# Where a head of the prompt's sparse attention ends and the next begins: last projection tile cut in two, query transposes and first scores moved into the next head's first tile

## What is computed

```python
def block(args):                     # _dsa_attention, one block of 128 queries
    qq, qqi, ww, qp = args
    rel = jax.nn.relu(jnp.einsum('bqhd,bsd->bqhs', qqi, ki).astype(jnp.float32))
    score = jnp.einsum('bqhs,bqh->bqs', rel, ww.astype(jnp.float32))
    score = jnp.where(vis[None], score, -jnp.inf)
    _, idx = lax.top_k(score, topk)
    ...
    s = jnp.einsum('bqngd,bqknd->bqngk', qq.reshape(b, qb, hkv, g, d), kg) * scale
    pr = jax.nn.softmax(jnp.where(ok[:, :, None, None, :], s, -jnp.inf), axis=-1)
    o = jnp.einsum('bqngk,bqknd->bqngd', pr.astype(v.dtype), vg)
ob = ob.reshape(b, t, D_B) * jax.nn.silu(gs)      # gate of each head, from the same input projection
```

## Time and profile before

| | us |
|---|---|
| median of three timed runs | 3538.22 |
| timed runs, lowest to highest | 3528.4 to 3543.82 |
| the profiled execution, its own time | 3525.9 |
| its span, first to last instruction | 3524.3 |
| TensorE busy in the span | 3332.7 (95%) |
| this stage, first product to the next stage's first | 1735.5 to 2491.3 |
| projections of this stage (line 1588), TensorE busy | 383.3 + 86.7 |

### The profile page before, as it was taken

One profiled execution on the slowest core, in us unless ns is written; L12 is line 12 of the kernel. 1 busy time (PEld: TensorE's weight loads), 2 busy tenths in 40 slices (PEclk: granted clock), 3 DMA queues, 4 the chain that ended last, 5 costly groups with the idle time before them and its releaser, 6 DMA issues. The chain is left out here.

```text
span 3524.3 us, 45823 instructions
## 1 busy us (share of the span) xinstructions
PE 3332.7 (95%) x17235; PEld 2281.7 (65%) x17265; DVE 1553.3 (44%) x2769; ACT 810.9 (23%) x1781; POOL 778.0 (22%) x992
## 2 busy tenths in 40 slices
PE   5878999999999999999999999999999998999999
PEld 3666777777777677777788888887444444444443
DVE  2025887878777787765434553112000023111111
ACT  4011233333425242433112222222100002000000
POOL 0005664646474655540000001000000000000000
PEclk8989999999999999999999999999999999999999
DMA  9866496878686877764301111103111023021010
GB/s 344 251 204 180 147 293 214 288 229 295 213 294 215 271 245 267 237 222 145 114 24 31 40 41 47 42 7 121 47 48 44 5 84 103 33 72 66 24 63 24
DMA packets 315102, 496.39 MB, mean 141 GB/s; under 512 B 26113, under 2 KB 211738, under 8 KB 313714
## 3 DMA queue, kind: packets, MB, share of 16 engines
q1 hardware_dynamic: 264512, 338.50, 30.1%
q0 software_dynamic: 46592, 146.84, 12.3%
q10 hardware_dynamic: 3778, 8.13, 0.6%
HBM read 466.02 MB, written 27.37 MB: 140 GB/s over the span
## 5 line engine op out<-in xcount | busy, mean ns | idle before, releaser
L1277 PE MATMUL Z<-W,hT 128*128 128x256 f32 x4608 | 1061.9, 385 | 16.7 <-DMA W<-in_w_in_dram 13.7
L1277 PEld LDWEIGHTS Z<-W,hT 128*128 128x128 f32 x4608 | 860.3, 191 | 173.8 <-issue 46.4
L2173 PE MATMUL S<-W,hT 128*128 128x512 f32 x1408 | 646.6, 597 | 1.8 <-SPq L2130 1.8
L2173 PEld LDWEIGHTS S<-W,hT 128*128 128x128 f32 x1408 | 265.1, 191 | 350.1 <-issue 347.3
L1588 PE MATMUL DB<-W,hT 128*128 128x256 f32 x1696 | 383.3, 381 | 0.0
L1588 PEld LDWEIGHTS DB<-W,hT 128*128 128x128 f32 x1696 | 316.3, 190 | 39.9
L996 DVE TENSOR_REDUCE sc<-big 128x16 f32<-128x1024 f32 x256 | 309.4, 1208 | 2.2 <-POOL big L816 1.7
L2173 PE MATMUL Z<-W,hT 128*128 128x512 f32 x640 | 303.6, 592 | 0.0
L992 DVE TENSOR_TENSOR big<-big,qb 128x1024 f32<-128x1024 f32 x160 | 231.8, 1449 | 76.4 <-DMA big<-in_cache_diff_k_dram 74.1
L816 POOL TENSOR_TENSOR big<-big,qb 128x1024 f32<-128x1024 f32 x96 | 231.3, 2410 | 101.9 <-DMA big<-in_cache_diff_k_dram 100.9
L2173 PEld LDWEIGHTS Z<-W,hT 128*128 128x128 f32 x640 | 121.5, 190 | 153.0 <-issue 152.6
(11 more groups left out here) (525 smaller groups left out, 3201.8 us busy)
## 6 DMA issues: line engine op xcount, KB each, us to landing
big<-in_cache_diff_k_dram POOLq DMA_DIRECT2D x256, 512.0 KB, 5.1
big<-in_cache_diff_v_dram SPq DMA_DIRECT2D x256, 512.0 KB, 4.6
W<-in_w_in_dram SPq DMA_DIRECT2D x27, 2048.0 KB, 9.9
W<-in_w_in_dram SPq DMA_DIRECT2D x52, 1024.0 KB, 8.1
W<-in_w_ple_gate_dram SPq DMA_DIRECT2D x16, 1024.0 KB
W<-in_w_out_dram SPq DMA_DIRECT2D x12, 1024.0 KB
kib<-in_cache_idx_k_dram POOLq DMA_DIRECT2D x256, 32.0 KB, 2.7
hT<-oT_d SPq DMA_DIRECT2D x3, 2048.0 KB, 20.4
```

The costliest lines, as they stand in the source:

```text
L1277: mm = pe.matmul(Z[b][:, 0:CW], hT[:, k, t * P:(t + 1) * P], W[:, w, k, :], start=(k == 0), stop=(k == KT - 1))
L2173: mm = pe.matmul(b, hT[:, k, t * P:(t + 1) * P], Wr[:, k, :], start=(k == 0), stop=(k == KT - 1))
```

## The change

Lists of three engines are written in a new order; no operation is added or taken away, and no semaphore. On TensorE:

- Tile 6 keeps only the first half of tile 7's projection; its two points `sample(point(s, 6, 0))` and `sample(point(s, 6, 1))` now follow each other. The second half stands in tile 7, behind `probabilities(H, 7, 0)`, and after it follow point, `probabilities(H, 7, 1)`, point, `output(H, 7)`.
- The next step begins with `half(s, 0, 0)`, then `queries(H)`, `turned(H - 1, 0)`, `half(s, 0, 1)`, `scores(H, 0)`, `turned(H - 1, 1)`, the point, `half(s, 1, 0)`, and only then the wait for the first exponentials, `probabilities(H, 0, 0)`, `scores(H, 1)`, `half(s, 1, 1)`, point, `output(H, 0)`.
- The last step (`s` = 8) has no next head, so these pieces stand there without the half tiles.

ScalarE takes tile 7 out of its bank in tile 7, between the two copies of probabilities, and copies the queries, the turned outputs and tile 0 before the first exponentials. VectorE rotates the queries in tile 7 between its two points, and makes the first maximum, the gates' product and point (s, 0, 0) ahead of the first tile.

```diff
-        ahead = lambda s, t: () if s == HB else ((t,) if s == 0 else ((0, 1) if t == 0 else ((t + 1,) if t < NT - 1 else ())))
+        ahead = lambda s, t: () if s == HB else ((0, 1) if t == 0 else ((t + 1,) if t < NT - 1 else ()))
...
-                for f in range(parts(t)):
-                    count_t += 1
-                    TN[s - 1, t, f] = count_t
                 if t == 0 and s >= 2:
                     for f in range(2):
                         count_t += 1
                         OG[s - 2, f] = count_t
+                for f in range(parts(t)):
+                    count_t += 1
+                    TN[s - 1, t, f] = count_t
...
                         half(0, t, f)
                         sample(point(0, t, f))
-                queries(0)
-                scores(0, 0)
                 for s in range(1, HB + 1):
                     H = s - 1
-                    for t in range(NT):
+                    if s < HB:
+                        half(s, 0, 0)
+                    queries(H)
+                    if s >= 2:
+                        turned(H - 1, 0)
+                    if s < HB:
+                        half(s, 0, 1)
+                    scores(H, 0)
+                    if s >= 2:
+                        turned(H - 1, 1)
+                    sample(point(s, 0, 0))
+                    if s < HB:
+                        half(s, 1, 0)
+                    pe.wait_ge(h_x, NT * H + 1)
+                    probabilities(H, 0, 0)
+                    scores(H, 1)
+                    if s < HB:
+                        half(s, 1, 1)
+                    sample(point(s, 0, 1))
+                    output(H, 0)
+                    for t in range(1, NT):
                         pe.wait_ge(h_x, NT * H + t + 1)
                         probabilities(H, t, 0)
                         if t < NT - 1:
                             scores(H, t + 1)
-                        elif s < HB:
-                            queries(s)
-                        if parts(t) > 1:
+                            if parts(t) > 1:
+                                probabilities(H, t, 1)
+                            if s < HB:
+                                half(s, t + 1, 0)
+                            sample(point(s, t, 0))
+                            if s < HB and t < NT - 2:
+                                half(s, t + 1, 1)
+                        else:
+                            if s < HB:
+                                half(s, t, 1)
+                            sample(point(s, t, 0))
                             probabilities(H, t, 1)
-                        if t == 0 and s >= 2:
-                            turned(H - 1, 0)
-                        for c in ahead(s, t):
-                            half(s, c, 0)
-                            if c != 1:
-                                sample(point(s, t, 0))
-                                if c == 0 and s >= 2:
-                                    turned(H - 1, 1)
-                            half(s, c, 1)
-                        if not ahead(s, t):
-                            if t == 0 and s >= 2:
-                                turned(H - 1, 1)
-                            sample(point(s, t, 0))
-                            if t == NT - 1 and s < HB:
-                                scores(s, 0)
                         sample(point(s, t, 1))
                         output(H, t)
...
                 gates(0)
-                queries(0)
-                exps(0, 0)
                 for s in range(1, HB + 1):
                     H = s - 1
+                    queries(H)
+                    if s >= 2:
+                        turned(H - 1, 0)
+                    if s < HB:
+                        take(s, 0)
+                    exps(H, 0)
+                    if s >= 2:
+                        turned(H - 1, 1)
                     for t in range(NT):
                         probabilities(H, t, 0)
-                        if t == 0 and s >= 2:
-                            turned(H - 1, 0)
                         if t == NT - 1 and s < HB:
-                            queries(s)
+                            take(s, t)
                         if parts(t) > 1:
                             probabilities(H, t, 1)
                         if t < NT - 1:
                             exps(H, t + 1)
-                        if t == 0 and s >= 2:
-                            turned(H - 1, 1)
-                        for c in ahead(s, t):
-                            take(s, c)
+                            if s < HB and t < NT - 2:
+                                take(s, t + 1)
...
                             gates(s)
-                            exps(s, 0)
...
                 rotate(0)
-                maximum(0, 0)
                 for s in range(1, HB + 1):
                     H = s - 1
+                    maximum(H, 0)
+                    silu(H)
+                    sample(point(s, 0, 0))
                     for t in range(NT):
                         dve.wait_ge(h_x, NT * H + t + 1)
                         link(dve.reciprocal(rrec[:, t, 0:1], rsum[:, t, 0:1]))
                         if t < NT - 1:
                             maximum(H, t + 1)
-                        if t == 0:
-                            silu(H)
-                        sample(point(s, t, 0))
+                        if t:
+                            sample(point(s, t, 0))
                         if t == NT - 1 and s < HB:
-                            maximum(s, 0)
+                            rotate(s)
                         sample(point(s, t, 1))
-                        if t == NT - 2 and s < HB:
-                            rotate(s)
                         output(H, t)
```

## The result

| | before | changed |
|---|---|---|
| median of four runs, us | 3535.55 | 3509.79 |
| lowest to highest, us | 3528.4 to 3543.82 | 3506.94 to 3512.67 |
| span of the profiled execution, us | 3524.3 | 3507.2 |

The ratio is 0.9931 (95% interval 0.991 to 0.9953): 25.8 us less between the medians, where 20 were forecast.

A forecast was written before the change was run, and what follows sets the result against it. TensorE, busy 95% of the span, bounds it; idle and half clock in the borders can be had. Border losses 48.8 less 29.6 give 19.2, plus 1 for the last: 3538.2 - 20 = 3518 us, range 3500 to 3534.

The forecast's parts named there:

- The cover: Between tile 7's second half and the queries, 5.8 us of TensorE work hides the rotation's 2.4; half tiles cover the exponential.
- border 1: Stretch into step 1 (border n: into step n), between heads' projection tiles; loss 8.1 us before, 0.3 after.
- Search points: Step 1, tiles 6 and 7: the second point waits for VectorE, 2.1 us in tile 6 and 1.6 in tile 7.
- HOT: Points of steps 2 and 3 needing eight one-hots from VectorE; new waits of 2.7 us each in tiles 6 and 7.
- point 77: Second point of step 4, tile 6, following point 76: a wait of 2.0 us for VectorE's work and two semaphores.
- Output: output(H, 7) stands behind the second probabilities and waits 0.85 us for their copy; steps 4 to 6 pay it.
- The clock: Half clock behind six new stalls of 2 us or more, charged 1.7 us each, bounds 0 and 3.4.
- rival B: New stalls come without half clock: the 10.2 us charged come back, gain 30, 3508 us; chance 0.18.
- Border 8: Last border, no half tile to put between: gain taken as 1 us, bounded by 2.3 above and -0.85 below.
- C: Each new stall costs 3.4 us of clock, the upper bound: gain 10, 3528 us; chance 0.13.
- D: Clock falls in tile 6's stall and stays down through the border: 41 us more, 3559 us; chance 0.04.
- E: The change fails and queries wait for the rotation as before, 12.2 us: gain 8, 3530 us; chance 0.05.

The follow-up runs named there:

- the second execution: The changed kernel run again with no edit: stage 732.25 us, 3516.28 us, ratio 0.9938 to the kernel before.
- the fillers: The changed kernel with products nobody reads put into the points' waits in tiles 6 and 7: stage 721.02 us, 3491.33 us, ratio 0.986 to before.
- the cut alone: The kernel before with only tile 7's second half moved into tile 7, right ahead of the queries: stage 775.32 us, 3553.84 us, ratio 1.0038.

## Why the prediction was right

**The cover.** Right, and shown by taking it away: the queries wait nowhere, not even the 0.3 us allowed for border 1, and baring the exponential gives back all that was gained. The waits for the exponentials went from 14.8 to 4.9 us, all of them the last head's, as told. That `half(s, 0, 0)` is needed for the rotation holds for border 1 only.

**The new waits.** Right in size. Search points: 1881.42 - 1879.28 = 2.14 us from start to start in tile 6, 2.0 without the point itself (2.1 forecast); in tile 7, from the end of the probabilities, 1891.07 - 1889.00 - 0.44 = 1.63 (1.6). HOT: 1973.15 - 1969.78 less the two points' 0.8 is 2.6 in tile 6; 1983.88 - 1979.96 - 0.44 less one point's 0.4 is 3.1 in tile 7, where half clock began during the point (2.7 each). Behind point 77: 2.18 idle (2.0). Output: 0.85 (0.85), new in borders 5 to 7 as told, and in border 8. The rows of the points' waits come to 9.4 us, a little under the 10 to 16 named as a sign, because small products that go at VectorE's pace count as busy.

**The clock.** Right in that half clock follows the points' waits and near in the sum, wrong border by border. Charged were 10.2 us: 1.7, 3.4, 3.4 and 1.7 in borders 2 to 5. Half of the half clock's length is again 10.2, and 12.0 in the second execution; by the fillers it was worth 1.66, 2.24, 4.51 and 0.01, in all 8.4. That the sums lie so near is luck in part, as misses cancel: border 5 had none, step 4's stall of 2.18 us left the clock at 1.00, and the border gained 1.31 where -0.6 stood, while border 4 had more than was charged. The term of border 5 was the largest miss that I can name, 1.7 to 1.9 us. Why 2.18 us there cost no clock while 1.30 us in step 2 did, I did not settle; with the cut alone, step 4 had a half clock stretch (2211.20 to 2214.61) where further waits for queries and scores followed.

Half clock began in or behind waits of 0.84 to 1.85 us here, in the HOT points together with 2.1 us of small products at VectorE's pace, and the filler's products took it away. The Trainium skill (TensorE: Matmul & The Clock Gate, "Why this matters for your kernels") warns of long idle gaps. By that alone rival B would have come, so the measurement decides against reading the warning as one for long gaps only.

**Border 8.** 2.17 and 2.44 us, not 1; the second lies over the bound of 2.3. The bound counted covers and left out the clock. Half clock in that border was 10.24 us before and is 3.41 now, which gives 3.4. TensorE's idle time in that period grew by 0.5 us, from 110.04 - 96.20 = 13.8 to 107.87 - 93.49 = 14.4; where the other 0.7 went stays open. The table load takes 1.28 us with 0.02 to the exponential, so no drain came here either (ScalarE, changed kernel):

```profile
2431.63 1.28 ACT L1776 ACT_TABLE_LOAD   x1
2432.93 0.37 ACT L1776 ACTIVATE e<-S,small 128x128 f32<-128x128 f32 x1
```

**The rest of the sum.** Borders 1, 6 and 7 gained 0.35 to 0.49 more than forecast, with no half clock left in them. In border 1, 0.3 of it is the wait that did not come; in the other two the work had been taken too long by some 0.4 us, and so the loss too small. Border 3 gained 1.5 more than forecast, of which 1.2 is its half clock (3.4 charged, 2.24 worth); border 4 gained 0.5 less, where its half clock took 1.1 more than charged. That leaves 0.3 and 0.6 us that I cannot lay to a step. In all 25.0 against 20.2: more by 1.9 in border 5, 1.5 in border 3, 1.3 in borders 1, 6 and 7, 1.2 in border 8 and 0.3 in border 2, less by 0.9 ahead of border 1 and 0.5 in border 4. In the second execution (23.5) borders 3 and 4 had 10.24 us of half clock each and gained 0.4 each, under the forecast.

**The base.** 3518 was worked out from a median of 3538.2; a fourth run brought it to 3535.55. Of the 8.2 us between forecast and result 2.7 come from there and 5.5 from the gain.

**The rivals.** B fell by the four half clock stretches and by the 8.4 us that the fillers gave back in their borders. Its 3508 lies nearer to the 3509.8 measured than the forecast's 3518, but by chance: half clock was there, and the distance is the base and the terms above. C fell by the stretches' length. D fell because each stretch ended ahead of its border's queries: border 4's last one at 2084.11 + 6.83 = 2090.94, its queries came at 2093.63. E fell with the row of the queries.

## What to carry to other kernels

Before moving a piece of work out of a gap, look at what it was covering where it stood: the half tile taken from between two points opened a wait there, and one order that covers both borders and points was worth as much again as the change. Price an idle wait in the middle of dense matmuls at more than its length: where the first exponential lost its cover, half clock cost 0.8 us more for each us of wait on average, and nothing in one border. Products that nobody reads were cheaper than the wait. Where the rest of a program varies by more than the change, compare the stage between two fixed products and not the spans.

## What the runs showed of the hardware

The stretches of half clock lasted 3.41, 6.83, 10.24 or 13.65 us (the last with the cut alone). Half clock is not the same in two executions of one order: 20.5 and 23.9 us in borders 2 to 4, from one more stretch behind the point of step 2, tile 6. The idle time alone does not tell where it comes: behind the second HOT point of step 2, tile 6, and its wait of 0.85 us, a stretch began in one execution and not in the other, and 2.18 us ahead of an output in step 4 were followed by none.
